# Three attentions worked on by pairs of heads

## What is computed

```python
# first block, each of 2 layers: 8 heads of 64, 2 key/value heads, all keys
s = jnp.einsum("bqhgd,bkhd->bhgqk", q_blk, k).astype(jnp.float32) * ATT_SCALE
p = jax.nn.softmax(s, axis=-1)
o = jnp.einsum("bhgqk,bkhd->bqhgd", p.astype(v.dtype), v)
# second block, layer 0: 16 heads, queries and keys of 96 (64 + 32 rotated), causal
s = jnp.einsum('bhqd,bhkd->bhqk', qi, kt).astype(jnp.float32) * scale
s = jnp.where(kpos[None, :] <= qpos[:, None], s, -jnp.inf)
p = jax.nn.softmax(s, axis=-1).astype(vt.dtype)
o = jnp.einsum('bhqk,bhkd->bhqd', p, vt)
# second block, layer 1: 3 groups of 16 heads of 64, windows of dilated tokens with a bias,
# the groups mixed by their logsumexp
```

## Time and profile before

| | us |
|---|---|
| median of 3 runs | 3962.08 |
| lowest, highest | 3959.38, 3965.43 |
| span of the profiled execution | 3963.9 |
| PE busy | 3824.6 (96%) |
| DVE busy | 2313.9 (58%) |
| ACT busy | 1311.5 (33%) |
| POOL busy | 814.3 (21%) |

### The profile page before, as it was taken

How to read it: one execution, slowest core, us unless ns; L and a number is a source line. 1 busy time by engine, 2 the same in 40 slices (tenths; PEclk the granted TensorE clock), 3 DMA queues, 4 the chain that set the end, 5 groups by cost and what they waited for, 6 DMA issues and landing times.

```text
span 3963.9 us, 48256 instructions
## 1 busy us (share of the span) xinstructions
PE 3824.6 (96%) x19316; PEld 3107.6 (78%) x19316; DVE 2313.9 (58%) x2995; ACT 1311.5 (33%) x1735; POOL 814.3 (21%) x580
## 2 busy tenths in 40 slices
PE   8998999999899999998999999999999999999999
PEld 6677888767788878886777888788877878777887
DVE  5987555497755555566667545633664554555434
ACT  4454232345433222223552222222233323332222
POOL 2100545210054435552113530000000000000000
PEclk9999999999899999998999999999999999999999
DMA  5112444311154435552213543233322122112331
GB/s 158 59 43 65 143 144 144 101 47 50 56 156 139 138 108 153 144 144 71 57 43 107 150 121 96 75 106 96 96 72 72 59 70 75 59 54 75 107 96 64
DMA packets 557161, 377.73 MB, mean 95 GB/s; under 512 B 30201, under 2 KB 554074, under 8 KB 556938
## 3 DMA queue, kind: packets, MB, share of 16 engines
q1 hardware_dynamic: 556938, 374.65, 32.3%
HBM read 372.44 MB, written 2.17 MB: 95 GB/s over the span
## 4 chain that ended last, share of the span: by engine, by line
PE 83%; DVE 13%; ACT 2%; issue 1%; SPq 0%; DMA 0%; DVEq 0%; ACTq 0%
PE bank L441 61%; PE bank L449 3%; PE bank L484 2%; PE bank L857 2%; DVE w_lo L419 2%; PE bank L2242 2%; PE bank L842 2%; PE bank L2267 1%; PE bank L478 1%; PE bank L479 1%; DVE conv_sum L1193 1%; PE bank L2288 1%; DVE hgrn_scores L1382 1%; DVE norm_tmp L1639 1%; PE bank L850 1%
## 5 line engine op out<-in xcount | busy, mean ns | idle before, releaser
L441 PE MATMUL bank<-H_hi,w_hi 128*128 128x512 f32 x2384 | 993.8, 417 | 3.0 <-DVE w_lo L419 1.3
L441 PE MATMUL bank<-H_hi,w_lo 128*128 128x512 f32 x2384 | 932.5, 391 | 0.0
L441 PE MATMUL bank<-H_lo,w_hi 128*128 128x512 f32 x2384 | 930.9, 390 | 0.0
L419 DVE TENSOR_TENSOR w_lo<-w_raw,w_hi 128x2048 fp32r<-128x2048 f32 (+3 forms) x285 | 732.0, 2568 | 141.0 <-ACT w_hi L410 124.3
L410 ACT ACTIVATE w_hi<-w_raw 128x2048 fp32r<-128x2048 f32 (+3 forms) x285 | 529.1, 1856 | 304.7 <-DMA w_raw<-in_ffn_w_up 133.6
L441 PE MATMUL bank<-U_hi,w_hi 128*128 128x512 f32 x1376 | 544.8, 396 | 3.4 <-DVE note L916 3.2
L441 PEld LDWEIGHTS bank<-H_hi,w_hi 128*128 128x128 f32 x2384 | 447.9, 188 | 125.8 <-issue 40.6
L441 PE MATMUL bank<-U_hi,w_lo 128*128 128x512 f32 x1376 | 537.6, 391 | 0.0
L441 PE MATMUL bank<-U_lo,w_hi 128*128 128x512 f32 x1376 | 536.3, 390 | 0.0
L441 PEld LDWEIGHTS bank<-H_lo,w_hi 128*128 128x128 f32 x2384 | 448.5, 188 | 100.3 <-issue 20.4
L441 PEld LDWEIGHTS bank<-H_hi,w_lo 128*128 128x128 f32 x2384 | 447.2, 188 | 97.6 <-issue 0.5
(11 more groups left out here) (370 smaller groups left out, 4926.6 us busy)
## 6 DMA issues: line engine op xcount, KB each, us to landing
w_mod_raw<-in_w_mod SPq DMA_DIRECT2D x144, 512.0 KB, 6.4
w_raw<-in_ffn_w_gate SPq DMA_DIRECT2D x88, 512.0 KB, 4.0
w_raw<-in_ffn_w_up SPq DMA_DIRECT2D x88, 512.0 KB, 5.3
w_raw<-in_dil_w_in SPq DMA_DIRECT2D x36, 1024.0 KB, 5.1
w_raw<-in_w_mlp_in SPq DMA_DIRECT2D x32, 1024.0 KB, 5.5
w_raw<-in_w_mlp_out SPq DMA_DIRECT2D x32, 1024.0 KB, 5.2
w_raw<-in_ffn_w_down SPq DMA_DIRECT2D x32, 1024.0 KB, 5.1
w_raw<-in_w_in SPq DMA_DIRECT2D x16, 1024.0 KB, 5.2
```

The lines of the kernel that those rows point to most:

```text
L419: dve.eng.tensor_tensor(WL[u % SLOTS][:, 0:n], RAW[u % SLOTS][:, 0:n], WH[u % SLOTS][:, 0:n].bitcast(F32), ALU.subtract).then_inc(lo_done. ...
L441: mm = pe.eng.matmul(bank[0:m, :], w[:, k, c0:c0 + m], r[:, k, :], start=(k == 0 and i == 0), stop=(k == kt - 1 and i == 2))
```

## The change

All three attentions now work on pairs: the same query block of two heads that share a tile, one in rows 0 to 63, the other in 64 to 127. Scores of the pair are written alternately, one head's into bank 4, the other's into bank 5 (3 and 4 in the third attention); with 64-row heads they also alternate between the row halves of the array. The padded keys, their copies and memsets are gone. Values are written alternately too, 64 columns each, one head into the lower, the other into the upper half of bank 3 (7 in the third). The division's product moves from VectorE to ScalarE, an ACTIVATE in place with the reciprocal as scale; VectorE keeps the reciprocal. There are four buffers of probabilities instead of three. The order of steps is new: pair j in scores, j-1 divided, j-2 multiplied by its values, and then both transposes of j-1. In the third attention the projection of 11 chunks uses three accumulation banks instead of four, and the last chunk's steps lie in 18 points beside three accumulations, not in 24 beside four.

```diff
-                mm.then_inc(s_ready.sem, s_ready.add())
+                pe.eng.wait_ge(p_ready.sem, p_ready.next(pe, 2, lag=2))
+                both = pairs_[i]["items"]
+                for n in range(len(both[0]["segs"])):
+                    for y in range(2):
+                        q, k, c0, add = both[y]["segs"][n]
+                        b, w = banks[4 + y], k.shape[-1]
+                        mm = pe.eng.matmul(b[:, c0:c0 + w], q, k, start=True, stop=add is None)
...
             elif kind == "values":
-                pe.eng.wait_ge(pt_seen.sem, pt_seen.next(pe))
-                if it["opens"]:
+                pe.eng.wait_ge(pt_seen.sem, pt_seen.next(pe, 2))
+                if pairs_[i]["opens"]:
                     pe.eng.wait_ge(o_used.sem, o_used.next(pe, lag=1))
...
+                for j in range(len(both[0]["v"])):
+                    for y in range(2):
+                        v, c0, start, stop = both[y]["v"][j]
+                        mm = pe.eng.matmul(banks[3][HEAD * y:HEAD * y + HEAD, c0:c0 + P], v, turned_probs(bufs, i, y)[:, j * P:(j + 1) * P], start=start, stop=stop)
                 mm.then_inc(pv_ready.sem, pv_ready.add())
...
+            elif kind == "divide":
+                for y, it in enumerate(pairs_[i]["items"]):
+                    act.eng.wait_ge(inv_ready.sem, inv_ready.next(act))
+                    for n, (_, k, c0, _) in enumerate(it["segs"]):
+                        c, part = it["stat"] + n, bufs["pr"][(2 * i + y) % 4][:, c0:c0 + k.shape[-1]]
+                        signal = pn_ready if n == len(it["segs"]) - 1 else act.step
+                        act.eng.activation(part, part, ACT.Identity, scale=RS[:, c:c + 1]).then_inc(signal.sem, signal.add())
...
+        def pair_steps(n, j):
+
+            steps_ = [("scores", j)] * (j < n) + [("divide", j - 1)] * (1 <= j < n + 1) + [("values", j - 2)] * (j >= 2)
+            return steps_ + ([("turn", 2 * j - 2), ("turn", 2 * j - 1)] if 1 <= j < n + 1 else [])
...
-                dve.eng.wait_ge(k_padded.sem, 2 * (l + 1))
-                ve.memset(Z[0:HEAD, ZK, :], 0.0).then_inc(dve.step.sem, dve.step.add())
...
+                        rows = slice(HEAD * y, HEAD * y + HEAD)
+                        keys = Z[rows, ZK, :] if y == kv else KSW[rows, :]
...
-                                  "none" if g or hq else "tiles")
+                                  "none" if g or hq else "tiles", acc=(0, 1, 2) if g or hq else (0, 1, 2, 3))
...
+            for j in range(n + 2):
+                steps_ += [("scores", j)] * (j < n) + [("values", j - 2)] * (j >= 2)
+                if 1 <= j < n + 1:
+                    steps_ += [("turn", 2 * j - 2), ("turn", 2 * j - 1)]
+                if g == 0 and hq and j < 3:
+                    steps_ += mixes[2 * j:2 * j + 2]
...
+                    for y in range(2):
+                        r = HEAD * y
+                        mm = te.matmul(banks[3 + y][:, c0:c0 + w], DQ[two][r:r + HEAD, t, b * P:(b + 1) * P], DK[two][r:r + HEAD, t, k1 - w:k1],
+                                       start=True, stop=True)
...
-                where = iter(dil_at(c, 48 if c < CHUNKS else 24))
+                where = iter(dil_at(c, 48 if c < CHUNKS else 18))
...
-                    pe_pair(pe, first, weave)
+                    pe_pair(pe, first, weave, 3)
```

More of the change, by code:

```diff
@@ L854, in att_pe_step @@
-                if it["opens"]:
+                pe.eng.wait_ge(pt_seen.sem, pt_seen.next(pe, 2))
+                if pairs_[i]["opens"]:
                     pe.eng.wait_ge(o_used.sem, o_used.next(pe, lag=1))
-                for j, (v, c0, start, stop) in enumerate(it["v"]):
-                    mm = pe.eng.matmul(banks[3][it["rows"], c0:c0 + P], v, bufs["pt"][i % 2 + (2 if i >= bufs["late"] else 0)][:, j * P:(j + 1) * P], start=start, stop=stop)
+                both = pairs_[i]["items"]
+                for j in range(len(both[0]["v"])):
+                    for y in range(2):
+                        v, c0, start, stop = both[y]["v"][j]
+                        mm = pe.eng.matmul(banks[3][HEAD * y:HEAD * y + HEAD, c0:c0 + P], v, turned_probs(bufs, i, y)[:, j * P:(j + 1) * P], start=start, stop=stop)
@@ L871, in att_act_step @@
             elif kind == "turn":
-                n = it["n"]
+                j, y = divmod(i, 2)
+                n = pairs_[j]["n"]
                 act.eng.wait_ge(t_ready.sem, t_ready.next(act))
-                act.eng.wait_ge(pv_twin.sem, pv_twin.next(act, lag=2))
-                act.eng.activation(bufs["pt"][i % 2 + (2 if i >= bufs["late"] else 0)][:, 0:n], banks[6][:, 0:n], ACT.Copy).then_inc(pt_ready.sem, pt_ready.add())
+                if y == 0:
+                    act.eng.wait_ge(pv_twin.sem, pv_twin.next(act, lag=1))
@@ L976, in mixer_at @@
                 put(p, step)
-            put(24, ("kpad", 0))
             put(36, ("vturn", 0))
@@ L980, in mixer_at @@
             put(50, ("gate", 1))
-            n, todo = ATT_HEADS * NB, []
-            for s in range(n + 3):
-                todo += [("scores", s)] * (s < n) + [("divide", s - 1)] * (1 <= s < n + 1) + [("turn", s - 2)] * (2 <= s < n + 2) + [("values", s - 3)] * (s >= 3)
+            n, todo = ATT_HEADS * NB // 2, []
+            for j in range(n + 2):
+                todo += pair_steps(n, j)
             for j, step in enumerate(todo):
@@ L1918, in mla_steps @@
                 return []
[L1919 to L1928 removed]
+            n, out = 3 * MLA_HEADS // 2, []
+            for j in range(6 * part - 6, n + 2 if part == 4 else 6 * part):
+                out += pair_steps(n, j)
             return out
@@ L1969, in mla_pe_step @@
             else:
-                if kind == "scores" and i % 12 == 0:
+                if kind == "scores" and i % 6 == 0:
                     pe.eng.wait_ge(mla_ready.sem, mla_ready.next(pe))
@@ L2266, in dil_pe_step @@
                         kb = b + 1 - w // P + x
-                        mm = te.matmul(banks[7][r:P, b * P:(b + 1) * P], DV[two][:, kb, h4 * HEAD:(h4 // 2 + 1) * P],
-                                       DT_[i % 2][:, c0 + x * P:c0 + (x + 1) * P], start=(x == 0), stop=(x == w // P - 1))
+                        for y in range(2):
+                            mm = te.matmul(banks[7][HEAD * y:HEAD * y + HEAD, b * P:(b + 1) * P], DV[two][:, kb, (h4 + y) * HEAD:(h4 + y + 1) * HEAD],
+                                           DT_[y][:, c0 + x * P:c0 + (x + 1) * P], start=(x == 0), stop=(x == w // P - 1))
                 mm.then_inc(dil_v.sem, dil_v.add())
```

284 lines of the change are left out of this document (126 added, 158 removed).

## The result

The changed kernel takes 4044.9 us (median of 4 runs, 4038.8 to 4049.3) against 3963.8 us (the kernel before again, now 4 runs): 1.0197 times, 95% interval 1.018 to 1.0214. Slower by 2%, where the forecast was faster by 2%. The profiled execution spans 4047.6 us (before 3963.9), +83.7.

A forecast was written before the change was run, and what follows sets the result against it. TensorE was taken to bound the kernel (83% of the span). Third attention -58, first -22, second +6 sum to -74 us; from the median 3962 that gives 3888 us, own range 3850 to 3925 (chance 0.64).

The forecast's parts named there:

- TensorE's work: All three attentions: paired half-array matmuls save TensorE 44 us in the first, 18 in the second, 66 in the third: 128.
- The rule against the row: Skill's strict program order for matmuls against a trace row of 16 factor-product records in 12 spacings; by the rule, 3902 us.
- The third attention: -58 forecast: Third attention: 66 us of TensorE's work saved, less 8 for logits ahead of factor products and the last chunk's projection.
- Steps that wait for each other lie 5 us and more apart, VectorE has half its time free, so 66 stay.: Third attention: no waits between steps hide the 66 us that TensorE's work shrinks by.
- The second: +6 forecast: Second attention: 24 rounds of 8.25 us make 198 against 192; TensorE's 18 us saved are gone in waiting; bounds -18 and +25.
- transpose from 3.3: Second attention: the first transpose of a round starts 3.3 us after the scores' end, behind exponentials and a division.
- 7.4: Second attention: length of a round in us, from trip, transposes, weights and 2.0 of scores; 0.85 added for other queued work.
- The first: -22 forecast: First attention: 11 us a layer gained over two layers, of 44 us that TensorE's work shrinks by; bounds 44 and 0.
- 3.9 us: First attention: trip from the scores' end through VectorE and ScalarE's exponentials and division back to TensorE, each round.
- the round closes at 7.6 us without any engine being late: First attention: a round takes 7.6 us, plus 0.4 for a tap under way: 8.0, where it was 8.75.
- The slower one: Rival, chance 0.04: the same round trip in 32 + 24 rounds of the first two attentions; with 2.8 us a round, 3990.
- 3.6 us of cover: First attention: TensorE's own work during the trip, 3.4 us of points and the values, with the scores' exit.

The follow-up runs named there:

- third_spread: The changed kernel with the third attention reordered: scores, values, then each head's exponential followed by the older pair's transposes for one head; 3992.0 us.
- heads_in_turn: The changed kernel with scores and values matmuls of the two heads one head after the other, not alternating, in all three attentions; 4046.6 us.
- mla_scalar: The changed kernel with third_spread's order; early attentions: values after the first exponential, divisions last, on ScalarE; the second's score heads in turn; 3906.6 us.
- divide_first: The changed kernel with a pair's division ahead of the next pair's scores in the first two attentions, still on ScalarE; 3970.5 us.
- values_ahead: mla_scalar with the values' step of the first two attentions put ahead of the first head's softmax again; 3967.6 us.
- two_moves: divide_first with the values of the older pair put between its two transposes' steps in the third attention; 3969.7 us.

## Why the prediction was wrong

The forecast was -74 us; measured were +81.

**TensorE's work: right.** Values 0.055, scores 0.053 and 0.43 for two, 0.10 for a visit's second record, as in the forecast. In third_spread TensorE is busy 542.7 us in the third, where it was 609.8: 67 saved, 66 forecast.

**The rule against the row.** The row stood: in heads_in_turn too TensorE starts one half's matmuls before all of the other's have started. The Trainium skill ("TensorE: Matmul & The Clock Gate", Part 3, The mechanism) has matmuls in strict program order; this trace disagrees with 12 spacings for 16 records.

**The third attention: -58 forecast, -3.8 measured. The step that failed** is "Steps that wait for each other lie 5 us and more apart, VectorE has half its time free, so 66 stay." The two transposes lie one step apart, 1.9 us where the chunk has most steps, and share a bank that ScalarE empties. I had asked how busy the engines are, not what stands ahead of the copy in ScalarE's order. 45 us more of waits and some 19 of slower clock ate the 66. In third_spread the change of the stage is within 3 us of the forecast one (617.5 to 562.2, -55).

**The second: +6 forecast, +44.7 measured.** The trip was right: "transpose from 3.3", measured 3.44 on average. What failed is the round made from it, "7.4" and 0.85 more, in which the scores and all other matmuls run at full speed. I wrote that the clock would fall and gave it no price. The stage took 232 us and not 198, and of these 34 some 22 are busy time (179 us, where the forecast's own work is 157): the same matmuls at a slower clock. The waits were only 12 us more than the forecast's own (198 less 157 is 41, measured 53).

**The first: -22 forecast, +29 measured (+36 with its first scores).** The trip of "3.9 us" is 3.74 in the undisturbed rounds. But it is 6 to 8.5 in five of 15, where a weight split of 1.5 to 2.3 us, twice VectorE's and three times ScalarE's, falls into it, and "the round closes at 7.6 us without any engine being late" was wrong: of 24.6 us of waits in layer one nearly half are for the division (11.5 us, 10 waits) and half for the copy (11.8 us, 6 waits of up to 2.7, four of them, 9.4 us, behind ScalarE's own weight split). The clock at 0.92 took more, with no term for it here either: TensorE is busy 133.5 us a layer, where mla_scalar does the same matmuls in 120.4 at 0.98.

**The rivals.** The slower one was the right mechanism, the round trip, for the first two stages, but its number (3990) was 55 too low: it left the third all of its 66 us, where 4 were measured. For the first two it had 56 x 2.8 - 62 = +95 us, more than the +74 measured, so its size is no hit either. At 0.04 it had far too small a chance: I had myself computed a trip of 3.9 us against 3.6 us of cover. That the division could be early and only stood in the wrong place in the list I did not see: the trip is not in the data, since a pair's exponentials are done a round before, but in the order of one engine's queue.

**Open.** The 7 us that are left outside the stages when the first attention's first scores are counted to it. Half of them lie between its end in layer one and its first scores in layer two: 549 us where it was 546, TensorE busy 525 us and not 521, at 0.96 and not 0.97; I ran nothing that isolates it.

## What to carry to other kernels

For each step that a hand-written order moves, write down every engine's own queue around it and ask what stands ahead of it there and what that waits for; a step whose inputs have long been ready is still as late as the wait in front of it. One step's place was worth 74 us here (divide_first), the wait for the values in front of a maximum about 60 (values_ahead against mla_scalar). And a wait of TensorE that comes in every round can cost more than its length, here 1.6 to 2.2 times (33 us of waits and 19 of slower matmuls in the third, 20 and 24 in the second), since the clock fell with it.

## What the runs showed of the hardware

- With waits of 0.3 to 3.9 us, 53 of 232 us in all, TensorE was at the lower of its two clock levels for 65 us, and its matmuls took 24 us longer (179 against 155 us busy, the change against divide_first, where 33 us are waits and 15 at the lower level). That the pairs themselves don't bring the clock down is shown by mla_scalar: the same matmuls at 0.97 to 0.99.
- The waits alone don't tell the clock. divide_first and two_moves have the same code in the first attention and wait 15 us each in its first layer; one is granted 0.93 and takes 145 us (130 busy), the other 0.98 and 138 (124 busy). What decided between them no run shows.
- Half-array matmuls of two column halves overlap even when the program has all of one half first: in x16 in 1.58 us the second half starts when five of the first half's eight records have started.
- A multiplication by one factor per row takes ScalarE 0.72 us for 128x512 (L888 in the changed kernel, mean of 25), VectorE 0.54.
